# Two transformer blocks in one kernel: gate matmuls moved one value block ahead, and the lower activation parts moved one step ahead on VectorE

## Chip, cores, metric

One core of one Trainium2 chip runs the whole program. The metric is the device time of one execution in microseconds, the median of several runs.

## What is computed

Two small transformer blocks run one after the other on 256 tokens of width 1024. The stretch that the change touches is the product-key expert layer ("peer") of the first model, which occurs twice (two layers). Of the reference this matters:

```python
def peer(xn, w_q, sub_keys, u, v):
    ...
    eidx = jnp.take_along_axis(cidx, pos, axis=-1)
    gate = jax.nn.softmax(top_s, axis=-1).astype(xn.dtype)
    ...
    def step(args):
        tc, ec, gc = args
        hid = jax.nn.gelu(jnp.einsum('td,thkd->thk', tc, u[ec]), approximate=False)
        return jnp.einsum('thk,thkd->td', gc * hid, v[ec])
```

Each token picks 8 x 16 of 16384 experts. The kernel gathers nothing: it computes the hidden value of every expert for every token, multiplies it by a gate (zero for experts not picked), and multiplies the result by the whole table v.

## The kernel before

**Numbers.** All large products are made to full float32 accuracy from three products of rounded numbers. A weight block of 128 x 1024 lands in one of 4 places of `ring`. ScalarE writes its rounded upper part (`whi`, L1085), GpSimd writes the rest, block minus upper part (`wlo`, L496). Both have 2 places. Activations are split in the same way: an upper part (`xh`) and a lower part (`xl`). TensorE then adds whi x xh, whi x xl and wlo x xh.

**The peer layer** has 128 rows of 128 experts. A row is a block. In the first part TensorE makes the hidden value of each block (`hidden`, 24 matmuls, L598 to L603) and ScalarE puts gelu of it into `hid` in `arena` (L1157). In the second part `down(j)` multiplies block j of v by row j of `hid` and adds into four PSUM banks: 4 matmuls whi x xh, 4 of whi x xl, 4 of wlo x xh, 128x512 each (L755). Rows are called j or k below.

**Gates.** Gates are made for 4 tokens at a time: 64 groups for each half of the 128 rows. VectorE writes one-hot tables for group j (`one_hots(j)`: L1576, L1578, L1580, all from SBUF operands in `aux`), TensorE multiplies them (`token_gates(j)`: 12 matmuls of 64 columns, L746, into `gen`), and VectorE multiplies `hid` of those tokens by the result (`gate_group(j)`, L1587). The gates of half 0 (rows 0 to 63) are made beside the hidden matmuls. Those of half 1 (rows 64 to 127) are made beside the value blocks 0 to 63: this is the stretch of the change, called the gate stretch below. Value blocks 64 to 127 follow without gates (the value stretch).

**What a value block needs.** Row k of `hid` is split by `chunk`: ScalarE writes its rounded upper part into one of 4 places of `xh` (L1183) and counts `hh_ready`. VectorE subtracts (`chunk_rest(k)`, L1565) into `xl` and counts `hl_ready`. `down(k)` waits for `hl_ready`, for `hi_ready` of its weight block, and between its second and third four matmuls for `lo_ready`.

**ScalarE's order** sets when the upper part of row k exists:

```python
def chunk(j, i=0):
    if j >= PAIR:
        rounded(v, j, i)
    if j >= RING:
        act.wait_ge(w_used, BASE[v] + j - RING + 1 + RING * i)
    act.activation(hid_hi[:, j % RING, :], hid[:, RING * i + j, :], ACT.Copy).then_inc(hh_ready, 1)
```

`rounded(v, k)` is the instruction of L1085 for block k. It waits until `hi_used` tells that the first eight matmuls of `down(k - 2)` are done (PAIR is 2). Before rows 64 to 127, ScalarE also waits until the last group of half 1 is gated.

**Order on the engines.** Every engine's order is written out by hand, in loops of 4 (`RING`). In the gate stretch TensorE does `token_gates(j)`, `down(j)`. VectorE does `one_hots(j + 1)`, `chunk_rest(j)`, `gate_group(j)`. `token_gates(j)` waits for `hot_ready` (from `one_hots(j)`) and `gated` of group j - 2. `gate_group(j)` waits for `tok_mm` (from `token_gates(j)`). SyncE loads the ring, GpSimd runs the subtractions of L496 in block order: each waits for its `whi` and for `down` two blocks earlier.

Of the kernel before, what the change touches and what calls it, by code (L numbers as in the profile page):

```python
# [29 lines left out]
RING = 4  # L30
# [14 lines left out]
HALF = NK // 2  # L45
# [118 lines left out]
def build(nc, dram, out):  # L164
    with ExitStack() as ctx:
# [396 lines left out]
        def _(pe):  # L562
# [15 lines left out]
            def acc_free():  # L578

                if au[0]:  # L580
                    pe.wait_ge(acc_out, au[0])
                au[0] += 1
# [23 lines left out]
            def fm_split(name, b, i=0):  # L606
                s, f = SPLIT[name] + b, FMBASE[name] + b

                if f >= 2:
                    pe.wait_ge(fm_out, f - 1 + RING * i)  # L610
                fm_passes(prod[:, f % 2, 0:T], s, i, RING)
# [99 lines left out]
            def peer(layer):  # L711
                turn(xn, KD, f"ffn{layer}")
                pe.wait_ge(fm_ready, FM[f"ffn{layer}"])
                pe.wait_ge(att_done, 2)
                for b in range(16):
                    fm_split(f"peer_q{layer}", b)

                for b in range(2):
                    pe.wait_ge(fm_out, FMBASE[f"peer_q{layer}"] + 8 * (b + 1))
                    w = arrive(BASE[f"peer_keys{layer}"] + b)  # L720
                    for x in range(NX):
                        for q in range(2):
                            bank = gen_bank()
                            for j in range(4):
                                n = 4 * q + j
                                mm = pe.matmul(bank[:, j * P:(j + 1) * P], peer_qT[:, 8 * b + n, x * P:(x + 1) * P],
                                               w[:, n * P:(n + 1) * P], start=True, stop=True)
                            mm.then_inc(gen_mm, 1)
                    pe.wait_ge(gen_mm, gi[0])
                    pe.nop().then_inc(w_used, 1)  # L730
                vs, hb = SPLIT[f"peer_v{layer}"], layer * NK
                tb = 2 * layer * HALF

                def hidden(i, j):
                    fm_split(f"peer_u{layer}", j, i)

                def token_gates(i, j, half):

                    n = tb + half * HALF + j
                    pe.wait_ge(hot_ready, n + 1 + RING * i)  # L740

                    if n >= 2:
                        pe.wait_ge(gated, n - 1 + RING * i)
                    for t in range(GTOK):
                        for g in range(PARTS):
                            mm = pe.matmul(gen[:, j % 2, t * HALF:(t + 1) * HALF], hot1[:, j % 2, :, t], hot2[:, j % 2, g, :, t],  # L746
                                           start=(g == 0), stop=(g == PARTS - 1))
                    mm.then_inc(tok_mm, 1)

                def down(i, j, first=False, last=False):  # L750

                    def values(w, h, start, stop):
                        for x in range(NX):
                            for n in range(2):
                                mm = pe.matmul(acc[:, 2 * x + n, :], h[:, j % RING, x * P:(x + 1) * P], w[:, n * 512:(n + 1) * 512],  # L755
                                               start=start, stop=stop, skip_group_check=True)
                        return mm

                    pe.wait_ge(hl_ready, hb + j + 1 + RING * i)
                    w = rounded(vs + j, i, RING)  # L760
                    values(w, hid_hi, first, False)
                    values(w, hid_lo, False, False).then_inc(hi_used, 1)
                    values(rest(vs + j, i, RING), hid_hi, False, last).then_inc(w_used, 1)


                with pe.Fori(0, HALF // RING - 2) as i:
                    for j in range(RING):
                        hidden(i, j)

                pe.wait_ge(normed, NORMED[f"route{layer}"])  # L770
                for x in range(NX):
                    bank = gen_bank()
                    for n in range(3):
                        mm = pe.transpose(bank[:, n * P:(n + 1) * P], sel_i[:, n, x, :], ident)
                    mm.then_inc(gen_mm, 1)
                for n in range(HALF - 2 * RING, HALF):
                    hidden(0, n)

                token_gates(0, 0, 0)
                with pe.Fori(0, HALF // RING - 1) as i:  # L780
                    for j in range(RING):
                        token_gates(i, j + 1, 0)
                        hidden(i + HALF // RING, j)
                for j in range(HALF - RING, HALF):
                    if j + 1 < HALF:
                        token_gates(0, j + 1, 0)
                    hidden(0, HALF + j)

                acc_free()
                for j in range(RING):  # L790
                    token_gates(0, j, 1)
                    down(0, j, first=(j == 0))
                with pe.Fori(1, HALF // RING) as i:
                    for j in range(RING):
                        token_gates(i, j, 1)
                        down(i, j)
                with pe.Fori(HALF // RING, NK // RING - 1) as i:
                    for j in range(RING):
                        down(i, j)
                for j in range(RING):  # L800
                    down(NK // RING - 1, j, last=(j == RING - 1))
            peer(0)

            turn(xn, KD, "mix1")
# [482 lines left out]
        def _(dve):  # L1287
# [246 lines left out]
            def peer(layer, last):  # L1534
# [27 lines left out]
                def chunk_rest(n, i):  # L1562

                    dve.wait_ge(hh_ready, layer * NK + n + 1 + RING * i)
                    dve.tensor_tensor(hid_lo[:, n % RING, :], hid[:, n + RING * i, :], hid_hi[:, n % RING, :].bitcast(F32),  # L1565
                                      ALU.subtract).then_inc(hl_ready, 1)

                for half in range(2):
                    before, chained = (2 * layer + half) * HALF, chain[0]

                    def one_hots(n, i=0):

                        tok = bass.ds(GTOK * n + GTOK * RING * i, GTOK)
                        if before + n:
                            dve.wait_ge(hot_ready, before + n + RING * i)
                        dve.tensor_tensor(hot, places[:, half * HALF:(half + 1) * HALF, :], wide(hk[:, 1, tok], 1, HALF),  # L1576
                                          ALU.is_equal).then_inc(v_chain, 1)
                        dve.tensor_tensor(hot1[:, n % 2, :, :], places, wide(hk[:, 0, tok], 1, NK), ALU.is_equal)  # L1578
                        dve.wait_ge(v_chain, chained + n + 1 + RING * i)
                        dve.tensor_tensor(hot2[:, n % 2, :, :, :], wide(hot, 1, PARTS), wide(hk[:, 2:2 + PARTS, tok], 2, HALF),  # L1580
                                          ALU.mult).then_inc(hot_ready, 1)

                    def gate_group(n, i=0):

                        dve.wait_ge(tok_mm, before + n + 1 + RING * i)
                        h = hid[:, half * HALF:(half + 1) * HALF, bass.ds(GTOK * n + GTOK * RING * i, GTOK)]
                        dve.tensor_tensor(h, h, gen[:, n % 2, 0:GTOK * HALF].rearrange("p (t c) -> p c t", c=HALF), ALU.mult)\  # L1587
                            .then_inc(gated, 1)

                    one_hots(0)  # L1590
                    dve.wait_ge(fm_out, FMBASE[f"peer_u{layer}"] + (half + 1) * HALF)
                    with dve.Fori(0, HALF // RING - 1) as i:
                        for j in range(RING):
                            one_hots(j + 1, i)
                            if half == 1:
                                chunk_rest(j, i)
                            gate_group(j, i)
                    for j in range(HALF - RING, HALF):
                        if j + 1 < HALF:
                            one_hots(j + 1)  # L1600
                        if half == 1:
                            chunk_rest(j, 0)
                        gate_group(j)
                    chain[0] += HALF
                with dve.Fori(HALF // RING, NK // RING) as i:
                    for j in range(RING):
# [395 lines left out]
```

## Time and profile before

| | |
|---|---|
| median of 3 runs | 3266.08 us (3265.84 to 3266.89) |
| span of the profiled execution, first to last instruction | 3265.0 us |
| TensorE matmul busy | 3029.1 us, 93% |
| GpSimd busy | 2136.7 us, 65% |
| VectorE busy | 1948.2 us, 60% |
| ScalarE busy | 1286.5 us, 39% |
| mean granted TensorE clock | 0.951 |
| gate stretch, first to 65th value block, layer 0 / layer 1 | about 234 / 236 us |

The profiled execution's span is 1.1 us under the median; of that execution nothing but the span is given. Busy time of TensorE counts modelled ends of overlapping matmuls, so "busy" there is not "at its peak": what counts below is the distance between starts. An idle time in brackets behind a row is that of the engine just before it, with the work that ended it.

### The profile page before, as it was taken

What the parts mean: (1) busy time and instruction counts of PE and PEld (TensorE: products, weight loads), DVE (VectorE), ACT (ScalarE), POOL (GpSimd) and SP (SyncE); (2) the same over time, 40 slices, a digit from 0 to 9 for tenths busy, and PEclk for the clock granted to TensorE, in tenths of its full rate; (3) what the DMA queues carried; (4) which work ended last, traced back from release to release, by engine and by line L of the source; (5) the groups of instructions that cost most, each with busy time, mean ns of one, the idle gap of its engine ahead of it and who ended that gap; (6) DMA issues with size and microseconds to landing.
All of it is one profiled execution on the core that took longest, in us unless ns stands there. A gap on an engine that the chain in (4) does not pass through costs nothing. (4 is left out here: it accounts for less than half of the span.)

```text
span 3265.0 us, 61411 instructions
## 1 busy us (share of the span) xinstructions
PE 3029.1 (93%) x21410; PEld 2710.7 (83%) x21410; DVE 1948.2 (60%) x2864; ACT 1286.5 (39%) x1734; POOL 2136.7 (65%) x887
## 2 busy tenths in 40 slices
PE   8889999999999889999999998978889899999996
PEld 7689999988877789999997776758688689999994
DVE  2429667778867673956777887765663642222224
ACT  3335544433344434554443334434400133333332
POOL 6469866666677676986666667756201368888883
PEclk9899999999999999999999999989678899999998
DMA  5245544444445454554444444544100345555553
GB/s 199 90 155 174 174 144 145 142 136 148 144 163 169 148 171 152 174 173 140 143 141 136 145 144 161 167 163 155 52 14 27 129 136 180 174 179 174 175 178 103
DMA packets 129783, 474.73 MB, mean 145 GB/s; under 512 B 14576, under 2 KB 14720, under 8 KB 129440
## 3 DMA queue, kind: packets, MB, share of 16 engines
q1 hardware_dynamic: 126864, 461.95, 44.1%
q0 software_dynamic: 2544, 11.41, 0.9%
q8 instruction: 59, 0.97, 0.1%
q14 instruction: 28, 0.23, 0.0%
q10 hardware_dynamic: 288, 0.17, 0.0%
HBM read 472.42 MB, written 1.05 MB: 145 GB/s over the span
## 5 line engine op out<-in xcount | busy, mean ns | idle before, releaser
L496 POOL TENSOR_TENSOR wlo<-ring,whi 128x1024 fp32r<-128x1024 f32 x863 | 2125.9, 2466 | 1106.2 <-ACT whi L1085 869.7
L1085 ACT ACTIVATE whi<-ring 128x1024 fp32r<-128x1024 f32 x863 | 918.3, 1064 | 1762.1 <-PE prod L599 612.6
L598 PE MATMUL prod<-xh,whi 128*128 128x256 f32 x3960 | 1000.1, 289 | 25.0 <-ACT gains L1075 9.8
L599 PE MATMUL prod<-xl,whi 128*128 128x256 f32 x3960 | 985.9, 286 | 0.0
L598 PEld LDWEIGHTS prod<-xh,whi 128*128 128x128 f32 x3960 | 773.5, 195 | 31.3 <-DVEq L1385 10.1
L599 PEld LDWEIGHTS prod<-xl,whi 128*128 128x128 f32 x3960 | 771.8, 195 | 1.7 <-issue 0.5
L603 PE MATMUL prod<-xh,wlo 128*128 128x256 f32 x3960 | 560.7, 285 | 10.2 <-POOL wlo L496 10.2
L603 PEld LDWEIGHTS prod<-xh,wlo 128*128 128x128 f32 x3960 | 515.4, 194 | 12.1 <-POOL wlo L496 12.0
L1576 DVE TENSOR_TENSOR aux<-aux 128x256 bf16<-128x256 bf16 x256 | 410.6, 1604 | 44.4 <-ACT arena L1157 36.8
L1565 DVE TENSOR_TENSOR xl<-arena,xh 128x256 fp32r<-128x256 f32 x256 | 354.4, 1385 | 102.7 <-ACT xh L1183 102.7
L755 PE MATMUL acc<-whi,xh 128*128 128x512 f32 x1024 | 298.4, 413 | 39.1 <-DVE xl L1565 38.0
L755 PE MATMUL acc<-whi,xl 128*128 128x512 f32 x1024 | 278.0, 393 | 0.0
L755 PE MATMUL acc<-wlo,xh 128*128 128x512 f32 x1024 | 275.6, 391 | 0.0
L755 PEld LDWEIGHTS acc<-whi,xh 128*128 128x128 f32 x1024 | 178.3, 189 | 101.0 <-ACT whi L1085 48.6
L746 PE MATMUL gen<-aux 128*128 128x64 bf16 x3072 | 233.1, 241 | 5.9 <-DVE aux L1580 5.9
L755 PEld LDWEIGHTS acc<-whi,xl 128*128 128x128 f32 x1024 | 194.0, 189 | 43.8
L755 PEld LDWEIGHTS acc<-wlo,xh 128*128 128x128 f32 x1024 | 193.7, 189 | 41.7
L746 PEld LDWEIGHTS gen<-aux 128*128 128x128 bf16 x3072 | 187.5, 119 | 45.0 <-issue 36.4
L1587 DVE TENSOR_TENSOR arena<-arena,gen 128x256 f32 (+1 forms) x256 | 107.7, 421 | 181.3 <-PE gen L746 181.3
L1885 DVE TENSOR_TENSOR arena<-arena,prod 128x512 f32<-128x512 f32 x32 | 22.0, 687 | 244.4 <-PE prod L603 244.4
L1580 DVE TENSOR_TENSOR aux<-aux 128x768 bf16<-128x768 bf16 x256 | 144.0, 562 | 0.0
L1893 DVE CAST mid_hi<-arena 128x512 fp32r<-128x512 f32 x32 | 14.2, 445 | 155.2 <-PE acc L1032 155.1
(289 smaller groups left out, 2702.5 us busy)
## 6 DMA issues: line engine op xcount, KB each, us to landing
ring<-in_peer_u SPq DMA_DIRECT2D x256, 512.0 KB, 3.5
ring<-in_peer_v SPq DMA_DIRECT2D x256, 512.0 KB, 3.5
ring<-in_exp_gate SPq DMA_DIRECT2D x64, 512.0 KB, 3.4
ring<-in_exp_up SPq DMA_DIRECT2D x64, 512.0 KB, 3.5
ring<-in_exp_down SPq DMA_DIRECT2D x64, 512.0 KB, 3.5
ring<-in_peer_q SPq DMA_DIRECT2D x32, 512.0 KB, 3.4
ring<-in_odd_in SPq DMA_DIRECT2D x24, 512.0 KB, 3.5
ring<-in_even_qk SPq DMA_DIRECT2D x16, 512.0 KB, 3.4
```

The lines of the kernel that those rows point to most:

```text
L496: pool.tensor_tensor(wlo[:, s % PAIR, :], ring[:, g % RING, :], whi[:, s % PAIR, :].bitcast(F32), ALU.subtract)\
L598: pe.matmul(dst, w[:, k * P:(k + 1) * P], xh[:, k, :], start=(k == 0), stop=False)
L599: mm = pe.matmul(dst, w[:, k * P:(k + 1) * P], xl[:, k, :], start=False, stop=False)
L603: mm = pe.matmul(dst, w[:, k * P:(k + 1) * P], xh[:, k, :], start=False, stop=(k == KD - 1))
L746: mm = pe.matmul(gen[:, j % 2, t * HALF:(t + 1) * HALF], hot1[:, j % 2, :, t], hot2[:, j % 2, g, :, t], start=(g == 0), stop=(g == PARTS - 1))
L755: mm = pe.matmul(acc[:, 2 * x + n, :], h[:, j % RING, x * P:(x + 1) * P], w[:, n * 512:(n + 1) * 512], start=start, stop=stop, skip_group_ ...
L1085: act.activation(whi[:, s % PAIR, :], ring[:, g % RING, :], ACT.Copy).then_inc(hi_ready, 1)
L1565: dve.tensor_tensor(hid_lo[:, n % RING, :], hid[:, n + RING * i, :], hid_hi[:, n % RING, :].bitcast(F32), ALU.subtract).then_inc(hl_ready, 1)
L1576: dve.tensor_tensor(hot, places[:, half * HALF:(half + 1) * HALF, :], wide(hk[:, 1, tok], 1, HALF), ALU.is_equal).then_inc(v_chain, 1)
L1580: dve.tensor_tensor(hot2[:, n % 2, :, :, :], wide(hot, 1, PARTS), wide(hk[:, 2:2 + PARTS, tok], 2, HALF), ALU.mult).then_inc(hot_ready, 1)
L1587: dve.tensor_tensor(h, h, gen[:, n % 2, 0:GTOK * HALF].rearrange("p (t c) -> p c t", c=HALF), ALU.mult)\
L1885: dve.tensor_tensor(mid, h_sig[:, e % 2, :], prod[:, 1, :], ALU.mult).then_inc(v_chain, 1)
```

## The change

In the gate stretch TensorE makes the gate matmuls of group j + 1 before value block j (so two groups stand before value block 0, and none before block 63). On VectorE `chunk_rest(0)` is made before the loop, and `chunk_rest(j + 1)` behind `gate_group(j)`, where `chunk_rest(j)` stood ahead of `gate_group(j)`. ScalarE, GpSimd and SyncE have the same instructions in the same order.

```diff
@@ TensorE, peer
                 acc_free()
+                token_gates(0, 0, 1)
                 for j in range(RING):
-                    token_gates(0, j, 1)
+                    token_gates(0, j + 1, 1)
                     down(0, j, first=(j == 0))
-                with pe.Fori(1, HALF // RING) as i:
+                with pe.Fori(1, HALF // RING - 1) as i:
                     for j in range(RING):
-                        token_gates(i, j, 1)
+                        token_gates(i, j + 1, 1)
                         down(i, j)
+                for j in range(HALF - RING, HALF):
+                    if j + 1 < HALF:
+                        token_gates(0, j + 1, 1)
+                    down(0, j)
                 with pe.Fori(HALF // RING, NK // RING - 1) as i:
                     for j in range(RING):
                         down(i, j)
@@ VectorE, peer
                     one_hots(0)
                     dve.wait_ge(fm_out, FMBASE[f"peer_u{layer}"] + (half + 1) * HALF)
+                    if half == 1:
+                        chunk_rest(0, 0)
                     with dve.Fori(0, HALF // RING - 1) as i:
                         for j in range(RING):
                             one_hots(j + 1, i)
+                            gate_group(j, i)
                             if half == 1:
-                                chunk_rest(j, i)
-                            gate_group(j, i)
+                                chunk_rest(j + 1, i)
                     for j in range(HALF - RING, HALF):
                         if j + 1 < HALF:
                             one_hots(j + 1)
-                        if half == 1:
-                            chunk_rest(j, 0)
                         gate_group(j)
+                        if half == 1 and j + 1 < HALF:
+                            chunk_rest(j + 1, 0)
```

VectorE, inside the loop of the gate stretch, with what each instruction waits for. Before (L1565 is `chunk_rest`, L1587 `gate_group`, L1576 to L1580 `one_hots`; an ISA row carries the wait of the row under it):

```order
L1576 ISA [waits hot_ready]
L1576 TENSOR_TENSOR aux<-aux 128x256
L1578 ISA
L1578 TENSOR_TENSOR aux<-aux 128x512
L1579 REGISTER_ALU
L1580 ISA [waits v_chain]
L1580 TENSOR_TENSOR aux<-aux 128x768
L1564 REGISTER_ALU
L1565 ISA [waits hh_ready]
L1565 TENSOR_TENSOR xl<-arena,xh 128x256
L1587 ISA [waits tok_mm]
L1587 TENSOR_TENSOR arena<-arena,gen 128x64x4
```

With the change (the same lines are now L1570, L1592 and L1581 to L1585):

```order
L1592 TENSOR_TENSOR arena<-arena,gen 128x64x4
L1569 REGISTER_ALU
L1570 ISA [waits hh_ready]
L1570 TENSOR_TENSOR xl<-arena,xh 128x256
L1580 REGISTER_ALU
L1581 ISA [waits hot_ready]
L1581 TENSOR_TENSOR aux<-aux 128x256
L1583 ISA
L1583 TENSOR_TENSOR aux<-aux 128x512
L1584 REGISTER_ALU
L1585 ISA [waits v_chain]
L1585 TENSOR_TENSOR aux<-aux 128x768
```

The wait for `hh_ready` stood behind the one-hot tables and now stands ahead of those of the next group.

TensorE, from the last hidden matmuls into the gate stretch of a layer. Before:

```order
L603 MATMUL prod<-xh,wlo 128x256 x8
L746 MATMUL gen<-aux 128x64 x12
L755 MATMUL acc<-whi,xh 128x512 x4
L755 MATMUL acc<-whi,xl 128x512 x4
L755 MATMUL acc<-wlo,xh 128x512 x4
L746 MATMUL gen<-aux 128x64 x12
```

With the change:

```order
L603 MATMUL prod<-xh,wlo 128x256 x8
L746 MATMUL gen<-aux 128x64 x24
L755 MATMUL acc<-whi,xh 128x512 x4
L755 MATMUL acc<-whi,xl 128x512 x4
L755 MATMUL acc<-wlo,xh 128x512 x4
L746 MATMUL gen<-aux 128x64 x12
```

Two groups of gate matmuls stand ahead of the first value block, and every later group is one value block further ahead.

## Rows read from the trace of the kernel before

**Rows 1.** Windows: gate stretch of layers 0 and 1, value stretch of layer 1.

```profile
core 0: us, PE busy (x) PEld busy (x) DVE busy (x) ACT busy (x) POOL busy (x), PEclk, DMA share, GB/s
672.00:905.70 233.70, 231.69 (x1524) 185.81 (x1524) 197.11 (x316) 87.71 (x128) 153.56 (x64) 0.99 0.44 141
1725.40:1961.80 236.40, 233.98 (x1524) 185.26 (x1524) 201.82 (x316) 87.78 (x128) 153.50 (x64) 0.99 0.43 140
...
1970.00:2157.00 187.00, 170.84 (x716) 131.65 (x715) 141.30 (x61) 82.01 (x120) 142.27 (x61) 1.00 0.51 167
```

**Rows 2.** Timeline (start, us, work), layer 1, two steps of the gate stretch.

```profile
1804.37 1.07 PE L755 MATMUL acc<-whi,xl 128*128 128x512 f32 x4
...
1805.53 1.07 ACT L1085 ACTIVATE whi<-ring 128x1024 fp32r<-128x1024 f32 x1 [2.09 <-issue]
...
1806.50 0.41 ACT L1183 ACTIVATE xh<-arena 128x256 fp32r x1
...
1806.76 2.47 POOL L496 TENSOR_TENSOR wlo<-ring,whi 128x1024 fp32r<-128x1024 f32 x1 [1.07 <-ACT whi L1085]
...
1807.11 1.18 PE L755 MATMUL acc<-whi,xh 128*128 128x512 f32 x4
...
1809.94 0.90 PE L746 MATMUL gen<-aux 128*128 128x64 bf16 x12
1810.10 0.41 DVE L1565 TENSOR_TENSOR xl<-arena,xh 128x256 fp32r<-128x256 f32 x1
...
1810.65 1.18 PE L755 MATMUL acc<-whi,xh 128*128 128x512 f32 x4
...
1811.67 1.09 PE L755 MATMUL acc<-whi,xl 128*128 128x512 f32 x4
```

**Rows 3.** Timeline, layer 1, two steps of the value stretch.

```profile
1981.76 1.08 PE L755 MATMUL acc<-whi,xl 128*128 128x512 f32 x4
...
1982.96 1.06 ACT L1085 ACTIVATE whi<-ring 128x1024 fp32r<-128x1024 f32 x1 [2.25 <-PE acc L755]
...
1983.93 0.40 ACT L1183 ACTIVATE xh<-arena 128x256 fp32r x1
1984.18 2.40 POOL L496 TENSOR_TENSOR wlo<-ring,whi 128x1024 fp32r<-128x1024 f32 x1 [1.22 <-ACT whi L1085]
...
1984.48 2.38 DVE L1565 TENSOR_TENSOR xl<-arena,xh 128x256 fp32r<-128x256 f32 x1 [1.24 <-ACT xh L1183]
...
1987.00 1.19 PE L755 MATMUL acc<-whi,xh 128*128 128x512 f32 x4 [0.52 <-DVE xl L1565]
```

**Rows 4.** Timeline, layer 1, start of the gate stretch.

```profile
1721.77 2.35 POOL L496 TENSOR_TENSOR wlo<-ring,whi 128x1024 fp32r<-128x1024 f32 x1 [0.49 <-ACT whi L1085]
...
1724.99 0.41 DVE L1565 TENSOR_TENSOR xl<-arena,xh 128x256 fp32r<-128x256 f32 x1
...
1725.46 1.84 PE L755 MATMUL acc<-whi,xh 128*128 128x512 f32 x4 [3.28 <-DVE xl L1565]
1725.66 0.28 DVE L1576 TENSOR_TENSOR aux<-aux 128x256 bf16<-128x256 bf16 x1
1725.86 0.41 DVE L1578 TENSOR_TENSOR aux<-aux 128x512 bf16<-128x512 bf16 x1
1726.20 0.55 DVE L1580 TENSOR_TENSOR aux<-aux 128x768 bf16<-128x768 bf16 x1
...
1730.62 1.17 PE L755 MATMUL acc<-whi,xh 128*128 128x512 f32 x4
```

**Rows 5.** Timeline, layer 1, end of the gate stretch.

```profile
1953.03 1.18 PE L755 MATMUL acc<-whi,xh 128*128 128x512 f32 x4
...
1956.83 0.42 DVE L1587 TENSOR_TENSOR arena<-arena,gen 128x256 f32<-128x256 f32 x1 [1.40 <-PE gen L746]
...
1957.89 1.06 ACT L1085 ACTIVATE whi<-ring 128x1024 fp32r<-128x1024 f32 x1 [5.06 <-DVE arena L1587]
...
1961.88 1.18 PE L755 MATMUL acc<-whi,xh 128*128 128x512 f32 x4 [2.30 <-DVE xl L1565]
```

## The prediction

> **What bounds the kernel now.** I read the windows first, to have the two gate stretches and a value stretch apart [rows 1]. In the gate stretches TensorE is busy 99% of the time (231.69 of 233.70 us, 233.98 of 236.40). GpSimd is busy 65 to 66% and ScalarE 37%. In the value stretch TensorE falls to 91% and GpSimd rises to 76%. The granted clock is 0.99 to 1.00 in all three, so the clock sets neither pace.
>
> Next the timeline of two gate steps, followed backwards from one value block [rows 2]. Call it k. The eight upper-part matmuls of block k - 2 end at 1804.37 + 1.07 = 1805.44: this is `hi_used`, time 0 of the chain. At 0.09 ScalarE starts the rounding of weight block k, at 1.06 the upper part of activation row k, done at 1.47. GpSimd starts on weight block k at 1.32 and ends at 3.79. VectorE subtracts row k at 4.66, takes 0.41 us and ends at 5.07. TensorE begins gate group k at 4.50 and value block k at 5.21 (1810.65). Its eight upper-part matmuls end at 1811.67 + 1.09 = 1812.76, that is at 7.32, and the chain begins anew. The reader is to see two things. Steps are 3.54 us where TensorE waits for nothing (1807.11 to 1810.65). And the upper part of row k is there at 1.47, only 3.7 us before it is used. It was never available earlier, because ScalarE rounds weight block k first, and that waits for `hi_used` of block k - 2. Over the stretch a step takes (1953.03 - 1730.62) / 61 = 3.646 us [rows 4, 5]. So TensorE's own order sets the pace, with about 0.1 us a step of waits.
>
> The value stretch shows what the same chain costs when VectorE must take row k as soon as it exists [rows 3]. Time 0 is 1981.76 + 1.08 = 1982.84. The upper part is done at 1.49. GpSimd starts at 1.34, VectorE at 1.64: 0.3 us too late. The subtraction takes 2.38 us instead of 0.41 and ends at 4.02, 0.28 us behind GpSimd's end (3.74). TensorE waits 0.52 us for it and starts block k at 4.16.
>
> So a VectorE instruction with two SBUF operands stands still while GpSimd's subtraction runs. The same holds in the gate stretch for whatever VectorE has next in that time; now it is the first table instruction of the following group, which has a step to spare.
>
> **What the change does.** It removes no work. Per layer it moves 63 of 64 gate groups ahead by one value block, and 64 subtractions of L1565 on VectorE. ScalarE, GpSimd and the loads keep instructions and order, so the upper part of row k still comes at 1.47 to 1.49. That is the point: `chunk_rest(k)` is asked for a step earlier, but its input is not there a step earlier.
>
> *The gate groups alone.* 12 matmuls take 0.71 us (1809.94 to 1810.65) [rows 2], before and after. Their number is unchanged: cost 0. They remove the wait of a value block for VectorE, at most 3.646 - 3.54 = 0.1 us a step.
>
> *The new wait.* On VectorE `chunk_rest(k)` now stands ahead of `one_hots(k + 1)`. TensorE needs the latter for gate group k + 1, which now stands ahead of value block k. So everything queued behind the subtraction is late: the three instructions of the one-hot tables, behind them `gate_group(k)`, and TensorE's gate group with the value block behind that. The chain from `hi_used(k - 2)` becomes:
>
> - Subtraction of row k ends: 4.02 us, as in [rows 3]. VectorE arrives early and waits for the row, as there. GpSimd has started 0.3 us before.
> - One-hot tables on free ports: 1726.20 + 0.55 - 1725.66 = 1.09 us [rows 4], less some 0.07 of overlap with the instruction ahead (1725.66 and 1725.86 are 0.20 apart where the first takes 0.28): 1.02.
> - From there to TensorE: 0.14, as from 1986.86 to 1987.00 [rows 3].
> - Gate group: 0.71. Value block k begins at 4.02 + 1.02 + 0.14 + 0.71 = 5.89, against 5.21 before.
>
> The rest of the chain (2.11 us to the next `hi_used`) is the same. A pair of steps thus takes 8.00 us instead of 7.32 in the same rows: 0.68 us more, 3.98 a step. There are 31 such pairs between the first and the 63rd block: 31 x 0.68 = +21.1 us a layer. Even and odd blocks make two such chains side by side. TensorE can do both, as it needs only 2 x 3.54 = 7.08.
>
> *The start.* Before, block 0 starts at 1725.46 [rows 4]. Now the subtraction of row 0 comes first, ends 0.28 us behind GpSimd's end (1724.12), thus at 1724.40. The tables of group 1 follow (1725.42), then gate group 1, and block 0 at about 1726.2: +0.8. After this long idle time the first step takes 5.16 us (1725.46 to 1730.62), 1.6 over 3.54, and four matmuls 1.84 instead of 1.18: TensorE runs slowly just then. Part of this slow time now passes in cheap gate matmuls, by my estimate 0.4 us. Net +0.4.
>
> *The end.* ScalarE may begin rows 64 to 127 only when the last group is gated. Before, that ends at 1957.25, its rounding starts at 1957.89 and block 64 at 1961.88, 8.85 us behind block 62 at 1953.03 [rows 5]. Now the last gate matmuls are a block earlier, and the last group is gated at about the time of `hi_used(62)`, 2.1 us behind block 62's start. With the same 0.64 and 3.99 us block 64 follows at 2.1 + 0.64 + 3.99 = 6.7: -2.1. The value stretch after it is the same, bound by its own chain.
>
> *Sum.* 21.1 + 0.4 - 2.1 = 19.4 a layer. The gate stretch of layer 0 is 2.7 us shorter than that of layer 1, but has the same form [rows 1], so it gets the same. Two layers: +38.8 us. On the span of 3265.0 this gives 3303.8. The median stands 1.1 higher: 3304.9, say **3305 us**, 1.2% slower.
>
> **Bounds.** The new order is nowhere in the trace. From below: if the one-hot tables cost nothing on the path, the chain is 6.98, TensorE's 7.08 rules, and the pair gains 0.24. From above: if GpSimd's next subtraction gets in between as well, a pair has up to 2.4 us more, and a layer up to 75. I take the value between, since each piece has its own row, and the nearest for the tables is that on free ports. Each pair may be off by 0.3 either way (the 0.14 is 0.06 in [rows 4], 1725.40 to 1725.46; a loop's edge may show): 31 x 0.3 x 2 = 19 us. That makes 3286 to 3324.
>
> **Rivals.**
> - *Faster: the slack is real.* If subtraction and tables are done when TensorE arrives, it works through at 3.54 a step: 62 x (3.54 - 3.646) = -6.6, with start and end -8.3 a layer, 3249 us. For it: TensorE is the busy engine (99%), and it is the wait that the change takes away. It decides if the tables are ready by 7.08 - 2.11 - 0.71 = 4.26 in the chain. They come at 5.04, and the upper part at 1.49 leaves GpSimd in front. Chance 0.05. Something between this and the forecast, within 0.2% of now: 0.03.
> - *Slower still: the tables are hit too.* The other chain's GpSimd subtraction starts at least 3.54 behind this one's, at 4.88. The last table instruction starts at 5.04 - 0.55 = 4.49, a margin of 0.4 us. If one pair in four is hit, 8 x 2.4 = 19 a layer, 3343 us in all. Against it: a longer pair moves the chains apart. Chance 0.06.
> - *VectorE first.* If VectorE takes the ports before GpSimd, the subtraction ends at 1.64 + 0.41 = 2.05, GpSimd runs from there to 4.45, and the tables, now stopped by it, end some 1.02 later, at 5.5 instead of 5.04: 0.46 x 62 = 28 us more, 3333. The Trainium skill, page "SBUF — State Buffer", section "SBUF: two separate sides", says that whichever of the two starts first has the shared ports for its whole instruction, so it allows both orders. The rows show VectorE 0.3 us behind and only the one order. Chance 0.03.
> - *The clock.* TensorE now waits in each step, 0.44 us. If it fell to its lower level in a quarter of the blocks, each would take about 2.4 us more (the four matmuls at 1725.46 are slower by 0.66 for three intervals, 0.2 each), +77 in all, 3382. Against it: waits of 0.52 us at every second block leave it at 1.00 [rows 1, 3]. Chance 0.02. The Trainium skill, page "TensorE: Matmul & The Clock Gate", knows kernels in which short, frequent idle times between matmul groups make the clock go up and down. No row here shows that.
>
> **How the numbers follow.** Forecast 0.81, the rivals as above. About 0.2% (6.5 us) is what a measurement of this kernel can tell from no change. Faster by more: 0.05; within: 0.03; slower: 0.92. The range is the forecast's own, widened by a few us for single hits of the tables: 3284 to 3328.
>
> **What would show it.** In the gate stretch: pairs of 8.0 us between starts of every second value block, of which one step near 3.54 and the other near 4.4; TensorE idle about 0.4 us a step ahead of the gate matmuls, not of the value block, ended by the last table instruction; the subtraction at 2.4 us instead of 0.41, waiting for ScalarE, and the first table instruction at 0.28 instead of 1.8; block 62 to block 64 in some 6.7 us; all other stretches as before. It is wrong if the subtraction stays at 0.4 us, or if TensorE's wait is ahead of L755.

## The result, and the profile after

The changed kernel takes 3301.95 us (median, 3300.25 to 3303.0), the kernel before 3266.16 us on the same chip. The ratio is 1.0108, with a 95% interval of 1.0094 to 1.0122: 1.1% slower. The forecast was 3305 us.

The windows of the kernel after, with the same stretches as [rows 1]; columns are window, length, busy time and count of each engine, granted clock, DMA share, GB/s:

```profile
core 0: us, PE busy (x) PEld busy (x) DVE busy (x) ACT busy (x) POOL busy (x), PEclk, DMA share, GB/s
672.90:924.40 251.50, 233.77 (x1516) 184.30 (x1513) 226.36 (x313) 87.65 (x128) 153.62 (x64) 0.99 0.39 131
1740.90:1996.00 255.10, 234.24 (x1516) 184.40 (x1513) 228.87 (x313) 87.65 (x128) 153.36 (x64) 0.99 0.39 129
2004.20:2191.20 187.00, 170.75 (x715) 131.61 (x715) 141.25 (x61) 82.00 (x120) 142.21 (x61) 1.00 0.50 167
```

TensorE has the same matmuls, and its gate stretches are 17.8 and 18.7 us longer (251.5 and 255.1 against 233.7 and 236.4). GpSimd's busy time is unchanged (153.6 against 153.6), VectorE's is 27 to 29 us more. The granted clock is 0.99 as before. The value stretch is the same, to 0.1 us of busy time.

The page's groups show who is late now. Two groups of the kernel after, then the same two of the kernel before; columns are line, engine, operation, operands, count | busy, mean ns | idle time before, and its releaser:

```profile
L1570 DVE TENSOR_TENSOR xl<-arena,xh 128x256 fp32r<-128x256 f32 x256 | 589.2, 2302 | 154.7 <-ACT xh L1188 154.3
...
L746 PE MATMUL gen<-aux 128*128 128x64 bf16 x3072 | 233.1, 241 | 49.3 <-DVE aux L1585 49.0
```

```profile
L1565 DVE TENSOR_TENSOR xl<-arena,xh 128x256 fp32r<-128x256 f32 x256 | 354.4, 1385 | 102.7 <-ACT xh L1183 102.7
...
L746 PE MATMUL gen<-aux 128*128 128x64 bf16 x3072 | 233.1, 241 | 5.9 <-DVE aux L1580 5.9
```

The subtraction (L1570, before L1565) takes 2302 ns where it took 1385, the first table instruction (L1581, before L1576) 952 where it took 1604. These are means over all 256 instructions, other stretches included. In the gate stretch of layer 1 alone the subtraction went from 0.41 to about 2.35 us, the first table instruction from about 1.7 to 0.28. TensorE's idle time ahead of the gate matmuls has grown from 5.9 to 49.3 us, of which 49.0 for the last table instruction (L1585). That ahead of the value blocks has fallen less, from 39.1 to 31.8. The chain itself, for the same block of layer 1 as in [rows 2] or one beside it, from the timeline (start, us, work, [idle before it and what ended it]):

```profile
1831.29 1.07 PE L755 MATMUL acc<-whi,xl 128*128 128x512 f32 x4
...
1832.49 1.07 ACT L1090 ACTIVATE whi<-ring 128x1024 fp32r<-128x1024 f32 x1 [3.07 <-PE acc L755]
...
1833.46 0.40 ACT L1188 ACTIVATE xh<-arena 128x256 fp32r x1
1833.71 2.39 POOL L496 TENSOR_TENSOR wlo<-ring,whi 128x1024 fp32r<-128x1024 f32 x1 [1.95 <-ACT whi L1090]
...
1834.02 2.37 DVE L1570 TENSOR_TENSOR xl<-arena,xh 128x256 fp32r<-128x256 f32 x1 [0.63 <-ACT xh L1188]
...
1836.31 0.28 DVE L1581 TENSOR_TENSOR aux<-aux 128x256 bf16<-128x256 bf16 x1
...
1836.85 0.55 DVE L1585 TENSOR_TENSOR aux<-aux 128x768 bf16<-128x768 bf16 x1
...
1837.31 0.41 DVE L1592 TENSOR_TENSOR arena<-arena,gen 128x256 f32 x1
...
1837.53 0.91 PE L746 MATMUL gen<-aux 128*128 128x64 bf16 x12 [0.70 <-DVE aux L1585]
...
1838.24 1.17 PE L755 MATMUL acc<-whi,xh 128*128 128x512 f32 x4
...
1839.25 1.08 PE L755 MATMUL acc<-whi,xl 128*128 128x512 f32 x4
```

`hi_used` of block k - 2 is at 1831.29 + 1.07 = 1832.36. The row is there at 1.50, GpSimd has started at 1.35, the subtraction waits for the row (the 0.63 in its bracket) and ends at 4.03, the tables at 5.04. TensorE starts the gate group at 5.17 after 0.70 us idle, the value block at 5.88, and the next `hi_used` is at 7.97. Start and end of the stretch, layer 1:

```profile
1736.00 0.90 PE L746 MATMUL gen<-aux 128*128 128x64 bf16 x12
...
1737.03 2.12 DVE L1570 TENSOR_TENSOR xl<-arena,xh 128x256 fp32r<-128x256 f32 x1 [3.71 <-ACT xh L1188]
...
1740.21 0.92 PE L746 MATMUL gen<-aux 128*128 128x64 bf16 x12 [3.31 <-DVE aux L1585]
...
1740.93 2.05 PE L755 MATMUL acc<-whi,xh 128*128 128x512 f32 x4
...
1746.94 1.18 PE L755 MATMUL acc<-whi,xh 128*128 128x512 f32 x4
```

```profile
1989.26 1.18 PE L755 MATMUL acc<-whi,xh 128*128 128x512 f32 x4
...
1990.95 0.41 DVE L1592 TENSOR_TENSOR arena<-arena,gen 128x256 f32<-128x256 f32 x1
...
1991.99 1.06 ACT L1090 ACTIVATE whi<-ring 128x1024 fp32r<-128x1024 f32 x1 [3.60 <-DVE arena L1592]
...
1996.01 1.18 PE L755 MATMUL acc<-whi,xh 128*128 128x512 f32 x4 [1.04 <-DVE xl L1570]
```

Block 0 starts 4.93 us behind the first gate group instead of 4.20 (1721.26 to 1725.46 before). Block 64 follows block 62 in 6.75 us instead of 8.85 [rows 5].

### The profile page after: what moved, and what is told of

The parts are those of the page before. It is cut to its first block and busy times, and to the rows that moved or that the text cites. A ratio compares the mean times of both kernels' runs of the same rounds, so it can differ in the third digit from the quotient of the medians.

```text
span 3298.5 us, 61389 instructions
## 1 busy us (share of the span) xinstructions
PE 3027.0 (92%) x21410; PEld 2706.8 (82%) x21410; DVE 2010.9 (61%) x2864; ACT 1286.5 (39%) x1734; POOL 2135.5 (65%) x887
## 5 line engine op out<-in xcount | busy, mean ns | idle before, releaser
L1570 DVE TENSOR_TENSOR xl<-arena,xh 128x256 fp32r<-128x256 f32 x256 | 589.2, 2302 | 154.7 <-ACT xh L1188 154.3
L755 PE MATMUL acc<-whi,xh 128*128 128x512 f32 x1024 | 296.3, 411 | 31.8 <-DVE xl L1570 31.8
L746 PE MATMUL gen<-aux 128*128 128x64 bf16 x3072 | 233.1, 241 | 49.3 <-DVE aux L1585 49.0
L1581 DVE TENSOR_TENSOR aux<-aux 128x256 bf16<-128x256 bf16 x256 | 243.8, 952 | 32.4 <-ACT arena L1162 29.4
L1592 DVE TENSOR_TENSOR arena<-arena,gen 128x256 f32 (+1 forms) x256 | 106.2, 415 | 116.2 <-PE gen L746 116.2
L1585 DVE TENSOR_TENSOR aux<-aux 128x768 bf16<-128x768 bf16 x256 | 144.3, 564 | 0.0
```

## Experiments

The theory is that two things together make the loss: the activation row is late, because ScalarE makes it behind the rounding of its weight block, and whatever VectorE has next is stopped by GpSimd's subtraction. The change put the one-hot tables behind the late row and gave TensorE an earlier need for them. "The lock" below is short for this: a table instruction or subtraction of VectorE stands still while GpSimd's subtraction runs. Rivals: one of the two orders costs by itself, or the lateness alone, or the lock alone.

**1. Only TensorE's half of the change.** The gate groups are ahead, VectorE's order is that of before. Against the changed kernel, the loop only:

```diff
+                            if half == 1:
+                                chunk_rest(j, i)
                             gate_group(j, i)
-                            if half == 1:
-                                chunk_rest(j + 1, i)
```

> TensorE's order of the change, VectorE's order of before (subtraction of row j behind the tables of group j + 1 and ahead of the gating of group j). Theory (late row ahead of the tables): the tables of group k + 1 no longer stand behind the subtraction of row k, so the pair of gate steps is TensorE's own 2 x 3.54 = 7.1 us instead of 7.96, and the time is 3266 - 0.1 x 62 x 2 - 2 for the end = about 3251 us (3247 to 3260). Rival (TensorE's order is what costs, through its wait for the gating of the group two back or for the tables a step earlier): gate steps of 3.9 to 4.0 us stay and the time is 3295 to 3305 us.

Measured: 3274.9 us (3271.1 to 3277.0), ratio 1.0027 (1.0017 to 1.0037). Neither theory had this. The half that was meant to help is slower than before, with a pair of 7.5 us in layer 1 (the mean from block 1 to block 62) where I expected 7.1. The timeline of a step of the gate stretch, layer 1:

```profile
1920.88 2.39 POOL L496 TENSOR_TENSOR wlo<-ring,whi 128x1024 fp32r<-128x1024 f32 x1 [1.44 <-ACT whi L1090]
1920.98 2.44 DVE L1581 TENSOR_TENSOR aux<-aux 128x256 bf16<-128x256 bf16 x1
...
1923.67 0.55 DVE L1585 TENSOR_TENSOR aux<-aux 128x768 bf16<-128x768 bf16 x1
...
1924.36 0.91 PE L746 MATMUL gen<-aux 128*128 128x64 bf16 x12 [0.22 <-DVE aux L1585]
```

Here the first table instruction (L1581) is the one that GpSimd stops, 2.44 us instead of 0.28. The tables end at 1924.22, 0.95 behind GpSimd's end, and TensorE, which needs them one block earlier than before, waits for them (0.22). So the lock on the tables alone costs, without a late row ahead of them. The chain in these rows is GpSimd's end at 3.74 after `hi_used`, then 0.95, 0.14, 0.72 for the gate group and 2.07: 7.6 us. In about every fourth step it is the second table instruction (L1583) that stands still, 2.62 us.

The stretch does not begin like this. In layer 1 the first two steps behind block 1 take 3.53 and 3.54 us. Then the last table instruction (L1585) is caught at 1740.61, 2.75 us for 0.55, and from there on the steps repeat 3.62, 3.80, 3.71 and 3.92. Experiments 2, 6 and 7 show the same kind of fall.

**2. Only VectorE's half of the change.** The subtraction is ahead of the next tables, TensorE's order is that of before. Against the changed kernel, the first of its loops:

```diff
-                token_gates(0, 0, 1)
                 for j in range(RING):
-                    token_gates(0, j + 1, 1)
+                    token_gates(0, j, 1)
                     down(0, j, first=(j == 0))
```

> VectorE's order of the change, TensorE's order of before. Theory: the row is still late and the subtraction still takes 2.4 us beside GpSimd, but the tables of group k + 1 are needed only after value block k, some 8 us behind the chain's start where they are ready at 5.0, so nothing waits: gate pair 7.1 us, time about 3252 us (3248 to 3262). Rival (VectorE's order costs by itself, whatever TensorE's is): gate steps near 3.9 to 4.0 us, 3295 to 3305 us.

Measured: 3261.6 us (3250.1 to 3270.0), ratio 0.9979 (0.9967 to 0.9991). By the median it does not cost, and the rival's 3295 to 3305 us falls. But the gain is a third of what I expected and the runs lie 20 us apart. In the profiled run layer 0 keeps 3.55 us a step throughout. Layer 1 keeps 3.53 for 28 steps behind block 1 and then takes about 3.87, near what the rival had for every step. Windows of its two gate stretches, whose columns are those above:

```profile
670.60:900.50 229.90, 227.99 (x1524) 184.24 (x1524) 200.06 (x318) 87.73 (x128) 154.41 (x64) 0.99 0.45 144
1718.60:1959.70 241.10, 234.70 (x1525) 185.09 (x1525) 231.78 (x318) 87.64 (x128) 162.97 (x64) 0.99 0.44 137
```

The timeline at the place where it falls from one pace into the other:

```profile
1818.97 2.40 POOL L496 TENSOR_TENSOR wlo<-ring,whi 128x1024 fp32r<-128x1024 f32 x1 [0.67 <-ACT whi L1085]
1819.04 2.75 DVE L1580 TENSOR_TENSOR aux<-aux 128x768 bf16<-128x768 bf16 x1
...
1826.27 2.49 DVE L1576 TENSOR_TENSOR aux<-aux 128x256 bf16<-128x256 bf16 x1
```

In the fast pace GpSimd stops the subtraction. At 1819.04 it stops the last table instruction (L1580) instead, 2.75 us for 0.55, VectorE falls behind, and from 1826.27 on the first table instruction (L1576) is stopped in 25 steps and the second (L1578) in 8, about every fourth.

**3 and 4. The row in time.** ScalarE makes the upper part of row k ahead of the rounding of block k, once on the changed kernel and once on the kernel before:

```diff
-                    if j >= PAIR:
-                        rounded(v, j, i)
                     if j >= RING:
 
                         act.wait_ge(w_used, BASE[v] + j - RING + 1 + RING * i)
                     act.activation(hid_hi[:, j % RING, :], hid[:, RING * i + j, :], ACT.Copy).then_inc(hh_ready, 1)
+                    if j >= PAIR:
+                        rounded(v, j, i)
```

> The change, and on ScalarE the upper part of activation row k made ahead of the rounding of weight block k instead of behind it. Theory: the row is then there right behind weight block k - 1, over 3 us earlier, the subtraction is done a step earlier, and neither the tables nor the value blocks of the value stretch wait: gate step 3.54, value step near TensorE's 2.75 instead of 3.14, time about 3204 us (3195 to 3225). Rival 1 (the lock and not the late row costs: a subtraction of 2.4 us ahead of the tables is too much whenever it begins): gate steps near 3.9 stay, about 3250 us or more. Rival 2 (the row's wait is not for the rounding): no change, 3302 us.

> The kernel before, with ScalarE's two instructions of a row swapped in the same way. Theory: gate step stays near 3.6 (the row was there in time), value step falls from 3.12 to near 2.75, time 3266 - 50 = about 3216 us (3208 to 3232). Rival: the value stretch is set by GpSimd's 2.4 us and its start behind each rounding, and stays at 3.1 us a step: 3266 us.

Measured: 3203.7 us on the change (3201.5 to 3214.8), ratio 0.9821 (0.9806 to 0.9836), and 3213.8 us on the kernel before (3212.4 to 3214.9), ratio 0.984 (0.9826 to 0.9854). Both as the theory had it (3204 and 3216). Windows of the two gate stretches and the value stretch of layer 1, swap on the change:

```profile
671.50:898.60 227.10, 227.10 (x1516) 183.77 (x1514) 200.50 (x313) 87.33 (x127) 153.62 (x63) 0.99 0.46 145
1693.70:1921.60 227.90, 227.90 (x1516) 184.33 (x1515) 204.37 (x313) 87.27 (x127) 154.20 (x63) 0.99 0.46 145
1923.00:2090.00 167.00, 167.00 (x738) 138.34 (x737) 146.43 (x62) 84.05 (x123) 147.54 (x62) 1.00 0.61 193
```

TensorE is recorded as busy in all of these 622 us. Value blocks start each 2.72 us (1995.10 and 1997.82 below), 5.44 a pair, where a pair took 6.27:

```profile
1995.10 1.07 PE L755 MATMUL acc<-whi,xh 128*128 128x512 f32 x4
...
1997.82 1.07 PE L755 MATMUL acc<-whi,xh 128*128 128x512 f32 x4
...
1998.33 2.40 POOL L496 TENSOR_TENSOR wlo<-ring,whi 128x1024 fp32r<-128x1024 f32 x1 [0.23 <-ACT whi L1090]
...
1998.63 2.38 DVE L1570 TENSOR_TENSOR xl<-arena,xh 128x256 fp32r<-128x256 f32 x1 [0.24 <-ACT xh L1186]
```

The subtraction still takes 2.4 us beside GpSimd; it is simply a block ahead. So the lock is no loss where there is a step to spare. In the gate stretch the swap takes the changed kernel from 255.1 to 227.9 us (layer 1), and the kernel before from 236.4 only to 233.8. Even this small gain is not in the steps, which stay at 3.58 and 3.74 us. It is at the end, where block 64 follows block 63 in 2.82 us instead of 5.28.

The order of the change, harmful before, is worth 5 to 6 us a layer once the row is in time (10 us between the medians).

**5. The lock made short.** The change with ScalarE's order untouched, and GpSimd's subtraction halved in the peer layers (the second half of each lower weight part is left over from earlier blocks, in the hidden products as well as in the value products). The edit, without the lines that choose it for these layers:

```diff
-pool.tensor_tensor(wlo[:, s % PAIR, :], ring[:, g % RING, :], whi[:, s % PAIR, :].bitcast(F32), ALU.subtract)
+pool.tensor_tensor(wlo[:, s % PAIR, 0:BLK // 2], ring[:, g % RING, 0:BLK // 2],
+                   whi[:, s % PAIR, 0:BLK // 2].bitcast(F32), ALU.subtract)
```

> The change, with GpSimd's subtraction cut to the first half of each block in the peer layers (the second half of the lower weight part is left over from earlier blocks, so the products with it are not the reference's). ScalarE's order is the change's, so the row is as late as there. Theory (late row and lock together make the loss): GpSimd's instruction takes about 1.2 us instead of 2.4, the chain of a gate pair falls from 7.96 to 6.8 and TensorE's 7.1 rules; the value pair falls from 6.28 to 5.1 and TensorE's 5.45 rules: about 3204 us (3195 to 3215). Rival (the late row alone makes the loss, GpSimd is only beside it): gate step stays at 3.9 to 4.0, 3290 to 3300 us.

Measured: 3184.9 us (3183.6 to 3187.3), ratio 0.9753 (0.9736 to 0.9769). The step of the gate stretch is 3.53 to 3.56, as the theory says, though the row is as late as in the change:

```profile
1807.38 1.29 POOL L500 TENSOR_TENSOR wlo<-ring,whi 128x512 fp32r<-128x512 f32 x1 [2.18 <-ACT whi L1095]
...
1807.68 1.27 DVE L1575 TENSOR_TENSOR xl<-arena,xh 128x256 fp32r<-128x256 f32 x1 [0.86 <-ACT xh L1193]
```

The subtraction waits for the row and is stopped again, but for 1.3 us. So the late row makes no loss when the lock is short. The time is 19 us under the forecast. By the two profiles this kernel is 16.8 us faster than experiment 3, and some 15 of that lie outside the value products (the first gate matmul, for instance, is at 422.5 instead of 427.2). Nearly all of it shows as TensorE's idle time: ahead of the hidden matmuls that read the lower weight part 0.0 us instead of 10.0 (in experiment 3 it ended with GpSimd's subtraction), and ahead of the gate matmuls 8.1 instead of 12.4.

**6 and 7. Either half with the row in time.** Each is experiment 1 or 2 with the edit of experiment 3.

> Gate groups ahead on TensorE, VectorE's order of before (the first of the two halves), and ScalarE's upper part of the row ahead of the rounding. Alone, the gates ahead gave a step of 3.77 us in layer 1. Theory A (there too a row that comes late is caught by GpSimd's subtraction and pushes the tables into the next one): with the row in time the step is 3.54, about 3204 us (3198 to 3212). Theory B (the tables are caught by themselves, the row has no part in it: end of the subtraction at 3.8, tables 0.95, signal 0.14, gate group 0.71, eight matmuls 2.1 make a pair of 7.6): step 3.77 stays, about 3275 - 52 = 3223 us.

> Lower part ahead on VectorE, TensorE's order of before (the second of the two halves), and ScalarE's upper part ahead of the rounding. Alone, this half had two paces, 3.53 and 3.87 us a step, in one execution. Theory A: with the row in time VectorE is a step ahead everywhere and the slow pace is gone: step 3.54, about 3204 us (3198 to 3212), as with the whole change. Theory B (the slow pace comes from a one-hot table caught by the lock, whenever the row comes): part of the steps at 3.87, 3210 to 3225 us and a spread of over 10 us between runs.

Measured: 3201.0 us (3199.3 to 3211.4), ratio 0.9799 (0.9783 to 0.9815), and 3203.7 us (3196.4 to 3214.5), ratio 0.9802 (0.9784 to 0.982). By the medians theory A, but the profiles show theory B's slow pace too. In both cases the profiled run is the slowest of the four (3211.4 and 3214.5 us). Gate stretches of 6, then of 7:

```profile
673.80:900.90 227.10, 227.10 (x1517) 184.09 (x1515) 199.64 (x314) 87.26 (x127) 154.04 (x63) 0.99 0.45 145
1695.80:1932.00 236.20, 232.96 (x1517) 184.45 (x1515) 226.03 (x314) 87.06 (x127) 153.19 (x63) 0.99 0.43 140
```

```profile
672.00:910.60 238.60, 233.87 (x1525) 184.89 (x1526) 228.54 (x318) 86.71 (x127) 161.35 (x63) 0.99 0.43 139
1705.80:1933.50 227.70, 227.68 (x1524) 184.09 (x1525) 205.42 (x318) 86.71 (x127) 152.60 (x63) 0.99 0.45 145
```

Both keep 3.54 or 3.55 a step in one layer and fall into the slow pace in the other (3.77 from the 23rd step on, 3.87 from the 30th). The slow steps of experiment 6 (3.62, 3.81, 3.72, 3.92) are those of experiment 1, so the late row has no part in that pace. But experiment 1 fell into it after two steps in either layer, experiment 6 in one layer only. It begins like this:

```profile
1775.89 2.59 POOL L496 TENSOR_TENSOR wlo<-ring,whi 128x1024 fp32r<-128x1024 f32 x1 [0.81 <-ACT whi L1090]
...
1776.15 2.75 DVE L1585 TENSOR_TENSOR aux<-aux 128x768 bf16<-128x768 bf16 x1
...
1779.48 2.52 DVE L1581 TENSOR_TENSOR aux<-aux 128x256 bf16<-128x256 bf16 x1
```

At 1776.15 GpSimd catches the last table instruction, and at 1779.48 the first one from its start. The pace does not go by the name of the instruction alone: in layer 0 of experiment 6, in the fast pace throughout, the first table instruction is stopped too, in 60 of 61 steps, but there it takes about 1.7 us, in the slow pace mostly 2.2 to 2.5, since in the fast pace VectorE comes to it later in GpSimd's run. A row in time makes the fast pace possible, it does not make it safe. Experiment 3 is in the fast pace in both layers of its profile, but its four runs (3201.5 to 3214.8) suggest that it can fall too; no profile of such a run was seen.

The stretches in the table are those of the profiled run, whose span is given; the time of a run is 1 to 3 us above its span.

| gate stretch, us (first to 65th block) | layer 0 | layer 1 | span of the profiled run, us | median, us |
|---|---|---|---|---|
| before | 233.7 | 236.4 | 3265.0 | 3266.2 |
| the change | 251.5 | 255.1 | 3298.5 | 3302.0 |
| 1: gates ahead alone | 238.6 | 241.0 | 3273.0 | 3274.9 |
| 2: lower part ahead alone | 229.9 | 241.1 | 3262.4 | 3261.6 |
| 3: change, row in time | 227.1 | 227.9 | 3199.8 | 3203.7 |
| 4: before, row in time | 232.4 | 233.8 | 3211.7 | 3213.8 |
| 5: change, short lock | 226.2 | 227.0 | 3183.0 | 3184.9 |
| 6: gates ahead, row in time | 227.1 | 236.2 | 3209.6 | 3201.0 |
| 7: lower part ahead, row in time | 238.6 | 227.7 | 3212.4 | 3203.7 |

Experiments 3, 6 and 7 beat the kernel before by 1.8 to 2.0% and the changed one by 3%. Between these three the runs show no difference. Most of that gain is in the value stretches: 2.72 us a block instead of 3.1, some 50 us in the two layers.

## Why the prediction was right, point by point

- *The pair of steps.* Forecast 8.00 us as 4.02 + 1.02 + 0.14 + 0.71 + 2.11. Measured 7.97 as 4.03 + 1.01 + 0.13 + 0.71 + 2.09, each part in the rows above. Over the stretch: from block 1 (1746.94) to block 62 (1989.26) 242.3 us, before 222.4, so 19.9 more, where the forecast had 21.1 (31 pairs of 0.68, one step more than these 61).
- *The form of it.* Steps alternate 3.55 and 4.40 in layer 1, TensorE idles ahead of the gate matmuls, and the table instruction releases it, as forecast. In the first steps both are near 3.9 and drift apart. The first of these steps was not forecast: GpSimd's first subtraction behind the long wait catches the first table instruction once in each layer (2.49 us at 1746.64, 2.48 at 678.61).
- *The start.* Forecast +0.8 for block 0, and -0.4 for slow time hidden in gate matmuls. Block 0 was 0.73 later, but the step from block 0 to block 1 took 6.01 us instead of 5.16: 0.85 more, not 0.4 less. The slow time was not hidden in the gate matmuls, it went on longer: in layer 1 the granted clock was 0.50, the lower of its two levels, through all twelve matmuls of block 0 (window 1740.9 to 1746.1), where it had risen to a mean of 0.83 by the last four before (1728.8 to 1729.9). In both kernels TensorE had been idle for 3.3 us shortly before. In layer 0 the step was not longer (5.86 after, 6.05 before), and over the nine traces of this document it lies between 4.58 and 6.05. So the 0.85 is scatter of this step as much as a cost of the change, and the estimate of 0.4 was not borne out.
- *The end.* Forecast -2.1, measured 6.75 against 8.85: -2.1.
- *Sum.* In layer 1: 0.73 + 0.85 + 19.9 - 2.1 = +19.4, just the forecast, but by luck: the start is 1.2 above its term and the steady part 1.2 below. Layer 0 grew by 18.6, its start included. The span grew by 33.5 where the sum had 38.8. Of the difference 0.7 is layer 0's gate stretch, 1.1 its value stretch, 2.8 lies between layer 0's last value block and layer 1's first gate group of this half, and 0.7 behind layer 1's last value block, the last two in code that nobody changed. Their cause is open, and one profile of each kernel cannot tell it from scatter.
- *Rivals.* "Faster, the slack is real" fell; experiment 3 shows what it lacked, a row one step earlier. "The tables are hit too" did not happen in the steady state of this kernel, though a hit on the last table instruction is just where experiments 1, 2, 6 and 7 fall out of the fast pace. The clock stayed at 0.99. "VectorE first" was not seen in the steady state.
- *A step that was incomplete.* I said TensorE's own order sets the pace of the kernel before, with small waits, and that the gate groups ahead would only remove these. The rows of the kernel before say otherwise, for the block at 1807.11:

```profile
1800.82 1.08 PE L755 MATMUL acc<-whi,xl 128*128 128x512 f32 x4
...
1803.29 2.40 POOL L496 TENSOR_TENSOR wlo<-ring,whi 128x1024 fp32r<-128x1024 f32 x1 [1.38 <-ACT whi L1085]
...
1804.05 1.79 DVE L1576 TENSOR_TENSOR aux<-aux 128x256 bf16<-128x256 bf16 x1
...
1806.56 0.41 DVE L1565 TENSOR_TENSOR xl<-arena,xh 128x256 fp32r<-128x256 f32 x1
...
1808.13 1.07 PE L755 MATMUL acc<-whi,xl 128*128 128x512 f32 x4
```

From `hi_used` at 1801.90 GpSimd's end comes at 3.79, the tables and the subtraction of VectorE 1.28 behind it, 0.14 to TensorE, and 2.09 to the next `hi_used`: 7.30 us, and the mean pair was 7.29. So the pair before is a lock chain as well, with the stopped table instruction at its head and no late row in it. Experiment 4 bears this out: with the row in time the pair stays as it was. In every second step TensorE's gate group begins 0.92 us ahead of the value block, not 0.71, which is the wait. Moving the gate groups ahead alone does not remove the chain, it makes it longer, 7.5 us (experiment 1). VectorE's order alone gives 7.07 in its fast pace and 7.74 in its slow one (experiment 2). The pair's growth of 0.68 is thus not a sum of two shares: it takes both orders together.

## What to carry to other kernels

Before work is moved a step ahead, look up when its input is made, not only when its result is wanted: here the producer on ScalarE stood behind a wait that nothing in the moved code showed, and swapping two instructions there was worth 1.6% to the kernel before and 3% to the changed one. Where a VectorE instruction stands still while GpSimd's runs, the pace is GpSimd's end plus all that VectorE must still do for the waiting engine, so count what stands behind the instruction that gets stopped. A schedule whose pace depends on which instruction is stopped, and for how long, can have two paces, and one profile does not tell which it will keep.

## What was not expected of the hardware

- The same loop ran at two paces in one execution, 3.53 and 3.87 us a step (experiment 2, and layer 0 of experiment 7), and 3.53 and 3.77 (experiment 6). Single runs of experiment 2 lay between 3250.1 and 3270.0 us, those of the kernel before between 3263.7 and 3269.9.
- Not every VectorE instruction is stopped. The gating (`gate_group`, L1587 or L1592), whose second operand `gen` lies in PSUM, never took more than 0.42 us in the gate stretches of these runs. In the kernel before it runs wholly inside a subtraction of GpSimd in 62 of layer 0's 64 steps. In the rows of the change above, 1837.31 for 0.41 us is one, beside GpSimd's from 1837.18 to 1839.64.
- GpSimd is held up as well. With a table instruction running when it starts, its subtraction took 2.73 us instead of 2.40, in the fast pace of experiment 2:

```profile
1797.73 0.55 DVE L1580 TENSOR_TENSOR aux<-aux 128x768 bf16<-128x768 bf16 x1
1797.81 2.73 POOL L496 TENSOR_TENSOR wlo<-ring,whi 128x1024 fp32r<-128x1024 f32 x1 [0.81 <-ACT whi L1085]
```

The last table instruction runs from 1797.73 to 1798.28. GpSimd's subtraction, begun at 1797.81, is 0.33 us longer than the 2.40 of others, most of the 0.47 us that were left of it. The Trainium skill, page "SBUF — State Buffer", section "SBUF: two separate sides", has both directions: the one that starts first keeps the shared ports and the other waits. The traces agree (2.75 for 0.55 us on VectorE, 2.73 for 2.40 on GpSimd). At the falls of experiments 1, 2 and 6 stands such an arrival: the last table instruction comes just behind GpSimd's start instead of ahead of it. That this alone sets off the fall is read from the rows and was not tested by an experiment.
